# A hybrid decoder layer on one Trainium2 core: mixer B's decode attention as TensorE matmuls

## The chip, the cores and the metric

The kernel runs on one core of one Trainium2 chip. The metric is the device time of one execution in microseconds. A measurement is the median of several executions. The engines are named as the profile names them: PE (TensorE), DVE (VectorE), ACT (ScalarE), POOL (GpSimd) and SP (SyncE, which here only issues transfers).

## The reference, cut to what matters

One layer is run for a prompt of 256 tokens and for 8 decode requests of one token each (264 token columns in all), in fp32.

```python
h = rms_norm(x, g_pre); qA,kA,vA,qB,kB,vB = h @ w_in       # 2048 -> 4352
# mixer A: 16 query heads, 2 kv heads, window 128, sinks
# mixer B: 16 heads of 64, keys at distances 0,d,2d,.. of three branches
DILATIONS = ((128, 1), (512, 4), (2048, 16))
# decode, per request n and head h:
s   = q . k_j / 8          # 320 cached rows and the own one
p   = exp(s - max)         # merged over the branches: a row in c branches counts c times
o_b = sum_j p_j v_j / sum_j p_j
x += rms_norm(concat(rms_norm(o_a), rms_norm(o_b)) @ w_out)
x += rms_norm((gelu(conv3(h2 @ w_gate)) * (h2 @ w_up)) @ w_down)
```

For decode, mixer B needs 8 requests x 16 heads x 321 rows of keys and of values, each row of 64 numbers. Every request and head has keys and values of its own, so there is one query for each set of keys. The count c of a row enters as a table T_MD that is added to the scores.

## The kernel before

**Tiling and stages.** Activations lie transposed: partitions are 128 features, columns the 264 tokens. Weights come as chunks of 128 x 1024 fp32 (512 KB) through a ring of four slots (`raw`). ACT casts a chunk to its high half `wh` (L502), DVE subtracts it to get the low half `wl` (L723), and PE multiplies three times (`mm3`, L1161 to L1163: wh·hh, wh·hl, wl·hh), 24 matmuls of 264 columns per chunk. Chunk n may be loaded when DVE has split chunk n-4. The first 68 chunks are w_in (17 groups of four), the next 16 the half of w_out for mixer B, then come the other half, gate and up, and down.

**The plan.** `make_plan` (driven by the table `STEP`) writes out by hand what happens after which chunk: `PLAN[n]` is a list of steps, and PE, ACT, DVE and POOL each run their part of those steps in that order, one after the other, after chunk n on PE (ACT is three chunks ahead with its casts, DVE two). SP runs the plan six chunks ahead (`AHEAD`), between its weight loads. All engines run their programs strictly in order, so a step that waits holds everything behind it on that engine. `evac` takes a finished group out of PSUM: for t = 0 to 3 the groups qB(t), kB(t), vB(t) (L732 to L735 rotate q and k; L783 scales v), then kvA and qA. `S`, `T`, `V` are the prompt's attention of one head: scores, transposes of the exponentials, times v.

**One bank for small steps.** PSUM bank `B_M` serves all steps listed in `MISC`; a step there waits until the step before it has been copied out (`take_misc`, `misc_free`).

**Mixer B's decode attention, before.** It is done in 8 units u = 2t + v, each of 128 features (two heads) for 8 requests.

- `qk` (PE L1199, ACT L532): q and k of the 8 decode columns are transposed and stored to DRAM (`q_dram`). SP reads q back, broadcast over 128 partitions, into `qb`, and writes the own key into row 64 of the third key block (`qI`, L432 and L434).
- `mul` (POOL L1073): `Kd` (128 rows x 3 blocks x 8 requests x 128 features) times `qb`, in place.
- `bS` (DVE L873): sum over each head's 64 features. `bT` (PE L1287, DVE L880, ACT L574, DVE L884 and L885): three transposes bring the scores to 16 rows x 321; mask, minimum, exponential, and the division.
- `pO`, `pI` (ACT L579, SP L444): the probabilities go to DRAM and come back broadcast over 64 partitions per head, into `Pb`.
- `bM` (POOL L1080, L1082): own value into `Vd`, then `Pb` times `Vd`. `bV` (ACT L585): eight passes with a running sum give `od`, the output by feature and request.

Keys and values come through SP's queue (`load_K` L450 and L451, `load_V` L457), between the weight chunks, and wait there for the step that frees their tile. `aload` (POOL) loads mixer A's caches once the last `bV` is over.

## Time and profile before

| | |
|---|---|
| runs | 1312.35, 1316.21, 1316.63 us; median 1316.21 |
| profiled execution | 1318.04 us, of which the span from first to last instruction is 1316.2 |
| PE busy | 1214.8 us, 92% of the span |
| DVE, ACT, POOL busy | 776.2, 571.0, 203.2 us |
| granted TensorE clock, mean | 0.955 |
| read from HBM | 231 MB, 180 GB/s over the span |

The page cuts the span into 40 slices of 32.9 us. From the 17th slice on PE is busy at 9 tenths or more of each, at full clock. Slices 3 to 16 (66 to 526 us) hold the plan's part and the turn to the FFN; there PE's busy share and its clock move up and down:

```profile
PE   5998777888989897999999999999999999999994
POOL 2053525260200020000101001010010000020003
PEclk9998978888978998999999999999999999999997
```

Each digit is a slice's busy share in tenths; PEclk is the granted clock in tenths of full speed. A busy PE in these rows means that a matmul is under way, not that it runs at its peak.

### The profile page before, as it was taken

What the parts mean: (1) busy time and instruction counts of PE and PEld (TensorE: products, weight loads), DVE (VectorE), ACT (ScalarE), POOL (GpSimd) and SP (SyncE); (2) the same over time, 40 slices, a digit from 0 to 9 for tenths busy, and PEclk for the clock granted to TensorE, in tenths of its full rate; (3) what the DMA queues carried; (4) which work ended last, traced back from release to release, by engine and by line L of the source; (5) the groups of instructions that cost most, each with busy time, mean ns of one, the idle gap of its engine ahead of it and who ended that gap; (6) DMA issues with size and microseconds to landing.
All of it is one profiled execution on the core that took longest, in us unless ns stands there. A gap on an engine that the chain in (4) does not pass through costs nothing.

```text
span 1316.2 us, 24517 instructions
## 1 busy us (share of the span) xinstructions
PE 1214.8 (92%) x9403; PEld 1186.3 (90%) x9403; DVE 776.2 (59%) x993; ACT 571.0 (43%) x938; POOL 203.2 (15%) x134
## 2 busy tenths in 40 slices
PE   5998777888989897999999999999999999999994
PEld 5987776787879897999999999999999999999994
DVE  5657859676554557655655556555565544454445
ACT  4334344436544456544444444444444433343331
POOL 2053525260200020000101001010010000020003
PEclk9998978888978998999999999999999999999997
DMA  6676969695522454455555555555555665656541
GB/s 252 224 242 222 295 195 285 204 255 155 150 75 82 139 172 117 146 184 183 170 168 188 184 182 169 167 189 185 180 171 166 216 185 179 177 181 184 176 144 66
DMA packets 83166, 237.03 MB, mean 180 GB/s; under 512 B 7432, under 2 KB 32368, under 8 KB 82032
## 3 DMA queue, kind: packets, MB, share of 16 engines
q1 hardware_dynamic: 81728, 232.30, 56.9%
q0 software_dynamic: 1072, 3.90, 0.9%
q8 instruction: 31, 0.51, 0.2%
q10 hardware_dynamic: 320, 0.20, 0.1%
q14 instruction: 15, 0.12, 0.0%
HBM read 231.13 MB, written 5.20 MB: 180 GB/s over the span
## 4 chain that ended last, share of the span: by engine, by line
PE 80%; DVE 8%; issue 3%; DMA 3%; ACT 3%; POOL 1%; SPq 0%; ACTq 0%; DVEq 0%; POOLq 0%
PE ps L1161 25%; PE ps L1162 24%; PE ps L1163 24%; DVE wl L723 2%; DMA raw<-in_w_in 2%; DVE bSc L873 1%; DVE bP L885 1%; PE ps L1225 1%; DMA Pb<-p_dram 1%; PE ps L1224 1%; ACT Pb L585 1%; PE ps L1233 1%; DVE sh L734 1%; POOL Kd L1073 1%; DMA qb<-q_dram 1%
## 5 line engine op out<-in xcount | busy, mean ns | idle before, releaser
L1161 PE MATMUL ps<-hh,wh 128*128 128x264 f32 x2080 | 609.3, 293 | 22.0 <-DVE wl L723 16.1
L1163 PE MATMUL ps<-hh,wl 128*128 128x264 f32 x2080 | 601.2, 289 | 0.0
L723 DVE TENSOR_TENSOR wl<-raw,wh 128x1024 fp32r<-128x1024 f32 x364 | 462.8, 1288 | 200.0 <-ACT wh L502 199.8
L1162 PE MATMUL ps<-hl,wh 128*128 128x264 f32 x1952 | 566.3, 290 | 0.0
L502 ACT CAST wh<-raw 128x1024 fp32r<-128x1024 f32 x364 | 375.4, 1045 | 356.9 <-PE ps L1163 298.5
L1161 PEld LDWEIGHTS ps<-hh,wh 128*128 128x128 f32 x2080 | 403.2, 194 | 31.7 <-DVE wl L723 17.5
L1163 PEld LDWEIGHTS ps<-hh,wl 128*128 128x128 f32 x2080 | 401.8, 193 | 0.0
L1162 PEld LDWEIGHTS ps<-hl,wh 128*128 128x128 f32 x1952 | 377.8, 194 | 0.2
L1162 PE MATMUL ps<-gl,wh 128*128 (+1 forms) x704 | 200.4, 285 | 0.0
L1161 PE MATMUL ps<-gh,wh 128*128 (+1 forms) x704 | 199.9, 284 | 0.0
L1163 PE MATMUL ps<-gh,wl 128*128 (+1 forms) x704 | 199.5, 283 | 0.0
L1162 PEld LDWEIGHTS ps<-gl,wh 128*128 128x128 f32 x704 | 132.6, 188 | 0.0
L1161 PEld LDWEIGHTS ps<-gh,wh 128*128 128x128 f32 x704 | 132.5, 188 | 0.0
L1163 PEld LDWEIGHTS ps<-gh,wl 128*128 128x128 f32 x704 | 132.4, 188 | 0.0
L1126 POOL COPY co<-U 128x4 f32 (+1 forms) x22 | 22.1, 1005 | 427.2 <-DVE U L985 427.2
L1073 POOL TENSOR_TENSOR Kd<-Kd,qb 128x3072 f32<-128x3072 f32 x8 | 55.3, 6912 | 59.8 <-DMA qb<-q_dram 59.7
L984 DVE TENSOR_TENSOR U<-ps,rB 128x512 f32<-128x512 f32 x22 | 15.2, 692 | 73.7 <-PE ps L1163 73.7
L1082 POOL TENSOR_TENSOR Pb<-Pb,Vd 128x2568 f32<-128x2568 f32 x8 | 47.3, 5908 | 72.1 <-DMA Pb<-p_dram 72.1
L1004 DVE TENSOR_TENSOR up<-ps,rB 128x528 f32<-128x528 f32 x22 | 15.6, 707 | 69.7 <-PE ps L1163 69.7
L678 ACT ACTIVATE cv<-U,par 128x280 f32<-128x280 f32 x44 | 25.0, 616 | 63.1 <-DVE U L985 63.1
L1233 PE MATMUL ps<-ident,Sm 128*128 128x128 f32 x96 | 18.4, 307 | 32.0 <-ACT Sm L544 31.9
L1142 POOL TENSOR_TENSOR up<-up,ysq 128x528 f32<-128x528 f32 x5 | 9.6, 1917 | 243.2 <-ACT ysq L710 242.7
(210 smaller groups left out, 1085.4 us busy)
## 6 DMA issues: line engine op xcount, KB each, us to landing
raw<-in_w_gate SPq DMA_DIRECT2D x88, 512.0 KB, 3.7
raw<-in_w_up SPq DMA_DIRECT2D x88, 512.0 KB, 4.6
raw<-in_w_down SPq DMA_DIRECT2D x88, 512.0 KB, 3.9
raw<-in_w_in SPq DMA_DIRECT2D x68, 512.0 KB, 6.9
raw<-in_w_out SPq DMA_DIRECT2D x32, 512.0 KB, 3.7
Pb<-p_dram SPq DMA_DIRECT2D x16, 642.0 KB, 8.5
Vd<-in_vb SPq DMA_DIRECT2D x8, 1280.0 KB, 8.5
Kd<-in_kb SPq DMA_DIRECT2D x8, 1024.0 KB, 5.9
```

What stands on the lines that cost most here:

```text
L502: nc.scalar.copy(wh[:, slot], raw[:, slot]).then_inc(hi_ready, 1)
L678: nc.scalar.activation(cv[:, k], U[:, k, 0:NU - 2], ACT.Identity, scale=par[:, bass.ds(i * 2 + (C_CW + k), 1)], bias=par[:, bass.ds(i * 2 ...
L723: V.tensor_tensor(wl[:, slot], raw[:, slot], wh[:, slot].bitcast(F32), ALU.subtract).then_inc(lo_ready, 1)
L984: line.do(V.tensor_tensor(U[:, :, 2:2 + SEQ], ps[:, g:g + 2, 0:SEQ], wide(rB[:, 0:SEQ]), ALU.mult))
L1004: V.tensor_tensor(up[:], ps[:, 2:4, 0:TOK], wide(rB[:]), ALU.mult).then_inc(up_taken, 1)
L1073: G.tensor_tensor(Kd[:], Kd[:], qb[:].unsqueeze(1).to_broadcast([P, 3, NDEC, P]), ALU.mult).then_inc(kq_ready, 1)
L1082: G.tensor_tensor(Pb[:], Pb[:], Vd[:], ALU.mult).then_inc(vp_ready, 1)
L1126: line.do(G.tensor_copy(co[:, bass.ds(i * 2, 2), 0:2], U[:, :, SEQ:SEQ + 2]))
L1161: nc.tensor.matmul(out, a, x, start=start, stop=False)
L1162: nc.tensor.matmul(out, a, xl, start=False, stop=False)
L1163: return nc.tensor.matmul(out, b, x, start=False, stop=stop)
L1233: ins = nc.tensor.transpose(ps[:, B_T, P * c:P * c + P], Sm[:, n % 2, P * c:P * c + P], ident[:])
```

## The change

Each unit's scores and outputs are computed by matmuls on PE, and no product is formed on POOL.

- Host arrays: keys now lie by feature (`kb`: 128 features x 8 requests x 321), values by row in three blocks (`vb`). Keys have two buffers (`Kt`), values one (`Vk`). Both loads are issued by POOL, not SP: `load_K(0)`, `load_V(0)`, `load_K(1)` at step `ss`, `load_K(u+2)` behind `bS(u)`, `load_V(u+1)` behind `bV(u)`.
- `qsel` (POOL): the own key is copied into column 320 of `Kt`; q goes into `Qsel`, a tile that is zero elsewhere. For request 4q + j there is a block of 32 columns in which column 0 holds head 0's q (upper 64 partitions zero) and column 1 head 1's.
- `bS` (PE): for q in 0, 1 and j in 0 to 3 one matmul whose stationary operand is that block (128 x 32) and whose moving operand is the keys of request 4q + j (128 x 321). Position j writes PSUM partitions 32j to 32j+31. q = 1 adds to q = 0: its columns sit two further (blocks are 130 apart, read 128 apart), so rows 32j to 32j+3 hold two requests of two heads. DVE masks and takes the minimum over 128 rows, ACT the exponential.
- `bR` (PE, ACT): three transposes of the 128 x 321 exponentials; copies to `pT`.
- `bV` (PE): for q, three row blocks and j, 24 matmuls: 32 probability columns stationary, the 128 features of request 4q + j's values moving, again at four column positions. ACT scales by the reciprocal sum while copying to `oR`.
- `bO` (PE, ACT): two transposes, then two small strided copies pick the wanted columns into `od`.
- `vdx` (PE, ACT, POOL): the decode columns of v are transposed, copied to `v8`, and sent by DMA into row 64 of the third value block (`load_vself`). It takes the place of `qk` and of the copy `vself`.
- Gone: `q_dram`, `p_dram`, `qb`, `Pb`, `qI`, `mul`, `bT`, `pO`, `pI`, `bM`, SP's part of the plan.

```diff
-    "qI": [-3, 2],
-    "mul": [-2, 4],
-    "bS": [2, 6],
-    "bT": [3, 11],
-    "pO": [3, 11],
-    "pI": [3, 12],
-    "bM": [7, 15],
-    "bV": [8, 16],
+    "qsel": [-3, -3],
+    "vdx": [1],
+    "bS": [-2, 3],
+    "bR": [0, 5],
+    "bV": [2, 7],
+    "bO": [3, 8],
...
             for n in range(4, N_IN):
                 load(chunk(n, 0, 4, 0), d["w_in"][GROUPS[n // 4][2], n % 4])
-                for s in PLAN.get(n - AHEAD, ()):
-                    stage(*s)
...
@@ scalar
+                elif kind == "bR":
+                    act.wait_ge(misc_ready, misc(kind, *a) + 1)
+                    line.do(nc.scalar.copy(pT[:, 0:256], ps[:, B_M, 0:256]))
+                    nc.scalar.copy(pT[0:65, 256:384], ps[0:65, B_M, 256:384]).then_inc(misc_free, 1)
                 elif kind == "bV":
-                    act.wait_ge(vp_ready, u + 1)
-                    for s in range(NDEC):
-                        ins = nc.scalar.activation(Pb[:, s], Pb[:, s], ACT.Identity, accum_out=od[:, 0, u, s:s + 1])
+                    act.wait_ge(misc_ready, misc(kind, *a) + 1)
+                    act.wait_ge(b_rec, u + 1)
+                    nc.scalar.activation(oR[:], ps[:, B_M, 0:256], ACT.Copy, scale=bri[u % 2]).then_inc(misc_free, 1)
...
@@ gpsimd
-                    G.tensor_tensor(Kd[:], Kd[:], qb[:].unsqueeze(1).to_broadcast([P, 3, NDEC, P]),
-                                    ALU.mult).then_inc(kq_ready, 1)
...
-                    G.tensor_tensor(Pb[:], Pb[:], Vd[:], ALU.mult).then_inc(vp_ready, 1)
...
+            def load_K(u):
+                G.dma_start(Kt[:, u % 2], d["kb"][u]).then_inc(Kt_landed[u % 2], 16)
+            def load_V(u):
+                G.dma_start(Vk[:, 0:2], d["vb"][u, :, 0:2]).then_inc(Vk_landed, 16)
+                G.dma_start(Vk[0:64, 2], d["vb"][u, 0:64, 2]).then_inc(Vk_landed, 16)
+            def load_vself(u):
+                v = u % 2
+                G.dma_start(Vk[64:65, 2], v8[:, P * v:P * v + P]).then_inc(Vk_full, 16)
...
@@ tensor
+                elif kind == "bS":
+                    u, = a
+                    pe.wait_ge(qsel_ready, 3 * (u + 1))
+                    take_misc(kind, *a)
+                    v = u % 2
+                    for q in range(2):
+                        for j in range(4):
+                            ins = nc.tensor.matmul(ps[32 * j:32 * j + 32, B_M, 0:KB],
+                                                   Qsel[:, v, P * q + 32 * j:P * q + 32 * j + 32],
+                                                   Kt[:, v, 4 * q + j], start=q == 0, stop=q == 1)
+                    ins.then_inc(misc_ready, 1)
...
+                elif kind == "bV":
+                    u, = a
+                    pe.wait_ge(Vk_landed, 32 * (u + 1))
+                    pe.wait_ge(Vk_full, 16 * (u + 1))
+                    take_misc(kind, *a)
+                    for q in range(2):
+                        for c, (k0, k1) in enumerate(KSPLIT_B):
+                            for j in range(4):
+                                ins = nc.tensor.matmul(ps[32 * j:32 * j + 32, B_M, P * q:P * q + P],
+                                                       pT[0:k1 - k0, P * c + 32 * j:P * c + 32 * j + 32],
+                                                       Vk[0:k1 - k0, c, 4 * q + j], start=c == 0, stop=c == 2)
+                    ins.then_inc(misc_ready, 1)
```

In the plan the numbers are chunks relative to e = 12t + 12, for v = 0 and 1. `vtr` stands at e + 1 too, ahead of `vdx`.

## Rows read from the trace of the kernel before

**Rows 1.** Table of stretches: us, PE, PEld, DVE, ACT, POOL busy, PEclk, DMA, GB/s.

```profile
25.00:320.00 295.00, 245.56 (x1720) 230.05 (x1718) 202.47 (x254) 123.94 (x299) 108.59 (x33) 0.90 0.76 232
57.07:236.69 179.62, 145.03 (x1041) 136.79 (x1040) 132.64 (x149) 72.93 (x173) 79.43 (x23) 0.90 0.82 246
236.69:314.21 77.52, 67.37 (x453) 61.87 (x450) 52.94 (x81) 38.08 (x107) 29.02 (x10) 0.87 0.74 223
```

**Rows 2.** Waits, 25 to 320 us: who <- for whom: us, times, longest.

```profile
ACT wh L502 <- DMA raw<-in_w_in: 36.7, 12, 10.6
PE ps L1233 <- ACT Sm L544: 31.9, 6, 8.8
PE ps L1250 <- ACT PT L552: 9.8, 4, 3.5
PE ps L1161 <- DVE wl L723: 2.1, 1, 2.1
```

**Rows 3.** Timeline, 211 to 224 us: start, us, instruction, [idle before].

```profile
212.07 6.71 POOL L1073 TENSOR_TENSOR Kd<-Kd,qb 128x3072 f32<-128x3072 f32 x1 [2.56 <-DMA qb<-q_dram]
212.16 7.18 DVE L734 SCALAR_TENSOR_TENSOR sh<-sh,tab 128x528 f32<-128x528 f32 x1
...
222.86 0.90 PE L1233 MATMUL ps<-ident,Sm 128*128 128x128 f32 x3 [8.80 <-ACT Sm L544]
```

**Rows 4.** Groups by line and shape, 25 to 320 us: xcount | busy, mean ns | idle before.

```profile
L723 DVE TENSOR_TENSOR wl<-raw,wh 128x1024 fp32r<-128x1024 f32 x57 | 91.9, 1620 | 27.8 <-ACT wh L502 27.7
...
L1073 POOL TENSOR_TENSOR Kd<-Kd,qb 128x3072 f32<-128x3072 f32 x8 | 55.3, 6912 | 59.8 <-DMA qb<-q_dram 59.7
L1082 POOL TENSOR_TENSOR Pb<-Pb,Vd 128x2568 f32<-128x2568 f32 x7 | 41.6, 5944 | 43.8 <-DMA Pb<-p_dram 43.8
...
L585 ACT ACTIVATE Pb<-Pb 128x321 f32<-128x321 f32 x56 | 25.5, 458 | 4.6 <-POOL Pb L1082 4.6
```

**Rows 5.** Table of stretches, two chunks behind a pause or small matmuls.

```profile
172.30:177.40 5.10, 5.10 (x28) 5.10 (x27) 1.22 (x1) 4.70 (x14) 0.00 (x0) 0.57 0.49 190
392.70:398.10 5.40, 5.40 (x25) 5.40 (x26) 0.58 (x2) 1.37 (x3) 0.00 (x0) 0.50 0.37 97
```

**Rows 6.** Timeline of PE, 113 to 122 us, one small step after another.

```profile
113.06 0.48 PE L1224 MATMUL ps<-ks,qs 64*128 64x128 f32 x2
...
113.91 0.39 PE L1161 MATMUL ps<-hh,wh 128*128 128x264 f32 x1
...
116.94 0.49 PE L1233 MATMUL ps<-ident,Sm 128*128 128x128 f32 x3
...
117.27 0.44 PE L1287 MATMUL ps<-ident,bSc 128*16 128x128 f32 x3
...
117.52 0.37 PE L1161 MATMUL ps<-hh,wh 128*128 128x264 f32 x1
...
120.53 0.33 PE L1250 MATMUL ps<-vn,PT 128*128 128x64 f32 x2
...
121.11 0.37 PE L1161 MATMUL ps<-hh,wh 128*128 128x264 f32 x1
```

**Rows 7.** Timeline, 126 to 128 us: v's transposes and ACT's copy of them.

```profile
126.07 0.66 PE L1209 MATMUL ps<-ident,vT 128*128 128x128 f32 x4 [1.75 <-DVE vself L784]
...
126.48 0.37 PE L1161 MATMUL ps<-hh,wh 128*128 128x264 f32 x1
...
126.76 0.59 ACT L521 COPY vn<-ps 128x512 f32<-128x512 f32 x1 [0.27 <-PE ps L1209]
```

**Rows 8.** DMA issues: out<-in, queue, xcount, KB each, median us from issue to landing.

```profile
Vd<-in_vb SPq DMA_DIRECT2D x8, 1280.0 KB, 8.5
...
VtA<-in_va POOLq DMA_DIRECT2D x1, 512.0 KB, 6.2
...
VtA<-vdec POOLq DMA_DIRECT2D x1, 4.0 KB, 3.3
```

**Rows 9.** The chain that ended last, in order of time: start, us, what.

```profile
113.54 0.43 PE ps L1225 x2
...
390.24 2.45 PE ps L1259 x32
```

More of the change, by code:

```diff
@@ L49 @@
 SUMS = MT // 2
-AHEAD = 6
 OUT_V = 5
@@ L144, in make_plan @@
         gap = STEP["gap"][t]
-        add(e + STEP["qk"][0], "qk", t)
         add(e + 1, "vtr", t)
+        add(e + STEP["vdx"][0], "vdx", t)
         for a in range(4):
@@ L194 @@
 MISC = [s for n in sorted(PLAN) for s in PLAN[n]
-        if s[0] in ("ss", "qk", "vtr", "vdec", "aS", "aT", "aR", "aV", "W", "ND", "bT")]
+        if s[0] in ("ss", "vtr", "vdx", "vdec", "aS", "aT", "aR", "aV", "W", "ND", "bS", "bR", "bV", "bO")]
 def number(kind, *args):
@@ L333, in build @@
         amn, al, aes, ari = (small[:, c:c + 1] for c in (74, 75, 76, 77))
-        bmn, bl, bri = (small[0:16, c:c + 1] for c in (78, 79, 80))
+        bmn, bl = (small[:, c:c + 1] for c in (78, 79))
+        bri = [small[:, c:c + 1] for c in (80, 81)]
         sinkn = small[:, 82:82 + H_A + 1]
@@ L365, in build @@
         KtA_landed, VtA_landed, VtA_full = sem("KtA_landed"), sem("VtA_landed"), sem("VtA_full")
-        Kd_landed, Kd_full, Vd_landed = sem("Kd_landed"), sem("Kd_full"), sem("Vd_landed")
-        q_out, qb_landed, p_out, Pb_landed = sem("q_out"), sem("qb_landed"), sem("p_out"), sem("Pb_landed")
-        kq_ready = sem("kq_ready")
-        bS_ready, bV_ready = sem("bS_ready"), sem("bV_ready")
-        vp_ready = sem("vp_ready")
+        Kt_landed = [sem(f"Kt_landed{c}") for c in range(2)]
+        Vk_landed, Vk_full = sem("Vk_landed"), sem("Vk_full")
+        qsel_ready = sem("qsel_ready")
         norm_a = sem("norm_a")
@@ L781, in evac @@
                         dve.wait_ge(v_stored, 16 * t)
-                        dve.wait_ge(misc_ready, misc("vtr", t - 1) + 1)
-                    line.step(V.tensor_tensor(vT[:], src, wide(rB[:]), ALU.mult))
-                    V.tensor_copy(vself[:, t], vT[:, :, SEQ:TOK]).then_inc(evac_done, 1)
+                        dve.wait_ge(misc_ready, misc("vdx", t - 1) + 1)
+                    V.tensor_tensor(vT[:], src, wide(rB[:]), ALU.mult).then_inc(evac_done, 1)
             def stage(kind, *a):
@@ L869, in stage @@
                     u, = a
[L870 to L876 removed]
                     dve.wait_ge(misc_ready, misc(kind, *a) + 1)
                     if u:
[L879 removed]
+                        dve.wait_ge(b_exp, u)
                     V.tensor_tensor_reduce(
[L881 removed]
+                        out=bSm[:], in0=ps[:, B_M, 0:KB], in1=tab[:, T_MD:T_MD + KB], scale=1.0, scalar=NEG,
                         op0=ALU.add, op1=ALU.min, accum_out=bmn).then_inc(misc_free, 1)
                     dve.wait_ge(b_exp, u + 1)
[L884 to L885 removed]
+                    V.reciprocal(bri[u % 2], bl).then_inc(b_rec, 1)
                 elif kind == "N":
```

194 lines of the change are left out of this document (85 added, 109 removed).

## The prediction

> **What bounds the kernel now.** I read the table of stretches first. In the 295.0 us from 25 to 320, where the w_in groups and mixer B's decode attention run together, PE is busy 245.6 us, so it sits idle 49.4 us at a granted clock of 0.90 [rows 1]. Afterwards the diff touches little. Next came PE's waits there: nearly all of the idle time ends with the exponential or the P^T copy on ACT (31.9 and 9.8 us), and ACT in turn sits 36.7 us until weights land [rows 2]. Neither is slow work. The timeline shows where ACT's delay starts: POOL's multiply of keys by q runs from 212.07 for 6.71 us, a rotate step on DVE that starts 0.09 us later takes 7.18 us, and PE then waits 8.80 us [rows 3]. So while POOL multiplies two SBUF tiles, a DVE instruction can stand still until it ends. The subtraction that makes the low weight half (L723) has a mean of 1620 ns in the stretch, a mix of free and held ones. POOL spends 55.3 and 41.6 us in the two multiplies [rows 4]. After such a pause PE also pays in clock: the chunk from 172.30 takes 5.10 us at a granted clock of 0.57, so mostly at 1.2 of the two levels 1.2 and 2.4 GHz [rows 5].
>
> How much is that together? A chunk (24 matmuls of 264 columns) at full clock goes from 117.52 to 120.53, 3.01 us. A head's S costs 0.85 (113.06 to 113.91), its T 0.33 (116.94 to 117.27), its V 0.58 (120.53 to 121.11), unit u's bT 0.25 (117.27 to 117.52) [rows 6]; four transposes (vtr; qk taken alike) 0.4 (126.07 to 126.48) [rows 7]. From 57.07 to 236.69 lie 36 chunks, 12 heads, 3 vtr and 3 qk, and 6 bT: 108.4 + 21.1 + 2.4 + 1.5 = 133.4 us. The window is 179.6, so 46.2 us are lost. From 236.69 to 314.21 lie 14 chunks, 8 S, 7 T, 7 V, 1.1 us of vtr and qk, and 3 bT: 57.1 of 77.5 us, 20.4 lost [rows 1]. **66.6 us** in all are idle time or low clock. PE's early wait for weights (2.1 us) [rows 2] I leave in place: before, keys and values go ahead of the weights in SP's queue, after it 3.9 MB (K0, V0, K1) share the engines with them from POOL's queue.
>
> **The change, part by part.** (1) *Multiplies, sums and broadcasts go.* POOL loses both multiplies, DVE the reduction bSc and the scaling of bP, ACT the eight accumulating passes per unit (25.5 us in seven units [rows 4]), the queues the broadcast reads of q and P. None of these engines is PE, so their own time is worth nothing; what they free is the 66.6 us. What is late next is PE itself, and I count the 66.6 in full: in a stretch without POOL's multiply on DVE's way (109 to 116) PE goes from chunk to chunk without a wait [rows 6].
>
> (2) *SP's queue* loses its waits (bS_ready, q_out, p_out, vp_ready), so weights no longer queue behind them: a gain that is part of (1). The loads themselves (two or three DMAs per unit, plus v's own row) go to POOL's queue, past its stores of k and v; nothing on POOL but its small copies waits behind them, and (6) prices the one that is late.
>
> (3) *PE's small steps.* Gone: 8 bT x 0.25 and 4 qk x 0.4, 3.6 us. New: 8 bR of three 128-column transposes x 0.33 (like T), 2.6; 8 bO of two x 0.22 (two thirds of that), 1.8; 4 vdx of two x 0.2, 0.8. Net **+1.6 us**.
>
> (4) *PE's big steps, where the trace has no such row.* bS is 8 fp32 matmuls of 321 moving columns, bV 24 of 128. An fp32 matmul leaves two records: two of 256 columns take 0.43 us on the chain [rows 9], 0.84 ns per column and record. One record of bS is then 0.27 us, one of bV 0.107. Upper end, if column positions do not run beside each other: 16 x 0.27 + 48 x 0.107 = 9.4 us per unit, 75.5 in all. Lower end, if all four run at once: a quarter, 2.35 per unit, 18.8 in all. Between them: the two records of one matmul stand next to each other in PE's order and use the same position, so the second must wait for the first, while the next position's first record can run beside the second. That gives (8 + 1) x 0.27 + (24 + 1) x 0.107 = 5.1 us per unit, **41** in all. A second row speaks for that size even if positions overlap fully: 32 records of only 16 columns take 2.45 us [rows 9], 77 ns each where streaming can't be the limit, and 48 such are 3.7 us for bV, with 1.2 to 2.4 for bS. I take 41.
>
> The Trainium skill, page "TensorEngine Tiling (Array Packing)", Tiling Modes, says that tiles operate independently and that different tiles execute weight loads and matmuls in parallel; by it the sum would hold the lower end. No row of before has a column position, so the trace neither agrees nor disagrees. "TensorE: Matmul & The Clock Gate", Part 3, gives 2.38x for three column positions, and says that matmuls start and end in program order, which is why I don't take the quarter.
>
> (5) *One bank for all of it.* B_M holds one small step at a time. vdx now follows vtr in the same plan step, so PE waits for ACT's copy, 0.59 us plus a hop [rows 7]: 0.75 x 4. bO(2t) is followed by bS(2t+1): two copies, 0.7 x 4. bR(7) by vtr(4): 0.75. Together **6.6 us**, and ACT's casts queue behind nothing new.
>
> (6) *v's own row.* load_vself(2t) is issued by POOL after vdx, one plan step before bV(2t) wants it on PE. The like DMA (4 KB from vdec) landed 3.3 us after issue [rows 8]; with copy, wait and issue 4.1 us after vdx, against a chunk of 3.01 and a head's S of 0.85 that PE has in between. It also stands in POOL's queue behind K(2t+2), 1.3 MB; 512 KB there took 6.2 us, the load before it included [rows 8], so I put 1.3 MB at some 9, and it was issued about 10 earlier. Bounds 0 (landed) and 4 us each; I take 1.5 x 4 = **6**. Queued behind the wait on PE are all chunks; POOL's wait for vdx holds only the next loads. Some of these waits end in a slow chunk, 2.1 us each [rows 5]: two of them, **4**.
>
> (7) *Hidden:* POOL's three small copies per unit (Qsel and the key column) lie a step ahead of bS; the memset of Qsel is over before x lands; DVE loses the memset of Kd; V and K prefetches have five or more chunks (over 15 us) against 8.5 us for the 1280 KB of Vd [rows 8]. If that cover failed, PE would wait 1 to 3 us per unit.
>
> Sum: -66.6 + 1.6 + 41 + 6.6 + 6 + 4 = **-7.4 us**. The profiled execution spans 1316.2 (1318.0 with what lies around it) and the median of the runs is 1316.2, so the same time: **1308.8 us**.
>
> **The rivals.** *A. Column positions don't overlap* (that the change doesn't do what it says): 34.5 us more than the forecast, 1343, slower. It decides above about 6.0 us per unit for bS and bV. For: fp32 streams at half the rate of the weight chunks' matmuls, so a limit in reading the operand may bind already. Against: nothing in the rows. *B. Full overlap:* 22 us less, 1287. Against: the 77 ns per record, and two records per matmul. *C. The clock falls behind the new stretches.* Behind the 2.45 us of 16-column matmuls the chunk from 392.70 took 5.40 us at 0.50, so 1.2 GHz [rows 5]. If a 32-wide stretch does the same, each of 16 costs 2 us: +32, 1341, slower. Against: the new matmuls stream 128 and 321 columns. *D. Weight loads at column positions aren't hidden.* "TensorE: Matmul & The Clock Gate", Part 3, says that weight loads overlap running matmuls only with another row group, and all positions here have the same. As a mechanism of this kernel: 64 records per unit that each wait for a load of about 77 ns [rows 9] add 4.9 us to the 9.4, so 39 us beyond rival A, 1382. The chunks speak against it: their loads, also all rows, are hidden in 24 matmuls per 3.01 us [rows 6].
>
> **How the numbers follow.** Forecast 0.44, A 0.20, B 0.21, C 0.12, D 0.03. The forecast's own range, 1297 to 1321, comes from (5) and (6) (6 to 29 us where I took 17) and from 4 to 6 us per unit in (4). The range reaches to B and A: **1285 to 1343**, which leaves out about half of A, D and a third of B. A measurement here tells 0.3%, 4 us, from no change. Faster: B 0.21 and two thirds of the forecast 0.30, 0.51. Same: 0.13. Slower: A, C, D and the rest, 0.36.
>
> **What would show it.** In the profile after: no DVE instruction stretched to 4 or more us before 320; PE idle there under 20 us instead of 49; bS of 2.4 us and bV of 2.7 between their first record and the next chunk (4.3 and 5.1 under A, 1.1 and 1.3 under B); PE's waits naming ACT's copies and Vk, each under 2 us; no slow chunk behind bS or bV (C). A chunk that waits for weights would mean that POOL's bulk loads crowd them out, and the 66.6 is then not all gained. It would be wrong above all if bS and bV take another time than 5.1 us per unit: each us there is 8 us.

## The result, and the profile after

After the change the kernel takes **1276.3 us** (median; 1274.8 to 1277.0) against 1314.3 (1312.0 to 1316.6) of the kernel before on the same chip: a ratio of 0.971, 95% interval 0.969 to 0.973. Two more series gave 0.969 (0.966 to 0.972) and 0.971 (0.968 to 0.974). The forecast of 1308.8 had the right sign and a fifth of the gain: 7 us were forecast, 38 measured, and the time lies below the range, nearest to rival B. The profiled executions span 1316.2 and 1274.7 us, 41.5 apart.

The table of stretches of the kernel after comes first (columns as in [rows 1]). The second row holds the same 50 chunks as the last two of [rows 1] together (57.07 to 314.21), counted from the start of the program: the first of them starts at 57.51 before and at 54.22 after.

```profile
25.00:320.00 295.00, 280.89 (x2468) 255.79 (x2467) 145.22 (x294) 127.22 (x276) 31.15 (x70) 0.98 0.59 200
54.22:279.55 225.33, 215.96 (x2014) 196.34 (x2012) 106.04 (x212) 96.10 (x212) 28.83 (x66) 0.99 0.64 213
```

Where the kernel before had PE idle for 49.4 of 295 us at a clock of 0.90, it is now idle for 14.1 at 0.98. What took 257.1 us (57.07 to 314.21) takes 225.3, although PE has all of the new matmuls in it. Two single chunks answer to [rows 5]: the one slow chunk that is left up to 279.55, at a clock of 0.66, and the chunk right behind the first scores, at full clock.

```profile
251.57:256.10 4.53, 4.53 (x28) 4.53 (x27) 1.23 (x1) 1.32 (x2) 0.00 (x0) 0.66 0.53 144
58.92:61.97 3.05, 3.05 (x29) 3.05 (x26) 2.19 (x5) 1.60 (x3) 0.53 (x1) 1.00 0.77 272
```

PE's waits, 25 to 290 us (who, for whom, us in all, times, longest), answer to [rows 2]:

```profile
PE ps L1262 <- ACT od L533: 3.6, 4, 1.7
PE ps L1172 <- ACT vn L466: 3.1, 4, 0.8
PE ps L1181 <- ACT pT L521: 1.8, 1, 1.8
PE ps L1295 <- DVE onat L829: 1.5, 1, 1.5
PE ps L1136 <- DVE wl L673: 1.4, 1, 1.4
PE ps L1205 <- ACT Sm L484: 0.6, 1, 0.6
PE ps L1281 <- issue: 0.5, 1, 0.5
PE ps L1262 <- POOL Qsel L1025: 0.4, 1, 0.4
```

The 31.9 us for the exponential are gone (0.6). The first three rows are waits for the bank B_M: bS (L1262) behind ACT's copy of the turned output, vdx (L1172) and vtr (L1181) behind ACT's other copies. The row for L1281 is bV of unit 4, at 178.77; no releaser is named for it, but it is v's own row: its DMA was issued at 175.18 and landed 3.5 us later, at 178.68. Two timeline rows show it, the first of POOL, the second of PE:

```profile
175.18 0.52 POOL L1067 DMA_DIRECT2D Vk<-v  x1 [6.30 <-ACT v L475]
...
178.77 0.38 PE L1281 MATMUL ps<-Vk,pT 128*32 128x128 f32 x5 [0.52 <-issue]
```

ACT's wait for weights (36.7 us in [rows 2]) and the group of the low weight half (1620 ns in [rows 4]) are, 25 to 320 us:

```profile
ACT wh L447 <- DMA raw<-in_w_in: 12.4, 4, 9.7
```

```profile
L673 DVE TENSOR_TENSOR wl<-raw,wh 128x1024 fp32r<-128x1024 f32 x64 | 77.5, 1219 | 21.0 <-ACT wh L447 20.9
```

1219 ns is the time of a subtraction that nothing holds up. The disputed cost, last: PE's timeline (start, us, instruction, in brackets the idle time before it) around the first scores and the first values.

```profile
57.70 1.29 PE L1262 MATMUL ps<-Kt,Qsel 128*32 128x321 f32 x16 [0.41 <-POOL Qsel L1025]
58.92 0.39 PE L1136 MATMUL ps<-hh,wh 128*128 128x264 f32 x1
...
74.07 1.52 PE L1281 MATMUL ps<-Vk,pT 128*32 128x128 f32 x48
75.52 0.39 PE L1136 MATMUL ps<-hh,wh 128*128 128x264 f32 x1
```

From the first record to the next chunk pass 1.22 us for scores and 1.45 for values, the same in all eight units: 2.67 us a unit, 21.4 in all, where the forecast had 41 and rival A 75.5. The values' matmuls alone (L1281; us, PE busy and records under way, PEld, clock) begin as a wave of four records, one for each position, and the next four join 0.11 us later:

```profile
74.06:74.17 0.11, 0.10 (x4) 0.10 (x8) 1.00 0.54 223
74.17:74.28 0.11, 0.11 (x8) 0.11 (x12) 1.00 0.92 372
```

### The profile page after: what moved, and what is told of

It is laid out like the page before. It is cut to its first block, busy times and chain, and to the rows that moved or that the text cites. A ratio compares the mean times of both kernels' runs of the same rounds, so it can differ in the third digit from the quotient of the medians.

```text
span 1274.7 us, 25414 instructions
## 1 busy us (share of the span) xinstructions
PE 1212.9 (95%) x9923; PEld 1178.8 (92%) x9923; DVE 692.5 (54%) x972; ACT 550.9 (43%) x850; POOL 118.0 (9%) x167
## 4 chain that ended last, share of the span: by engine, by line
PE 91%; DVE 3%; issue 2%; ACT 1%; POOL 0%; DVEq 0%; ACTq 0%; POOLq 0%
PE ps L1136 28%; PE ps L1137 27%; PE ps L1138 27%; PE ps L1197 1%; PE ps L1196 1%; PE ps L1281 1%; PE ps L1205 1%; PE ps L1262 1%; PE ps L1165 1%; PE ps L1318 1%; PE ps L1224 1%; PE ps L1223 1%; DVE yT L980 1%; DVE yT L981 1%; PE ps L1222 0%
## 5 line engine op out<-in xcount | busy, mean ns | idle before, releaser
L1136 PE MATMUL ps<-hh,wh 128*128 128x264 f32 x2080 | 602.2, 290 | 20.7 <-DVE wl L673 14.9
L1137 PE MATMUL ps<-hl,wh 128*128 128x264 f32 x1952 | 559.4, 287 | 0.0
L673 DVE TENSOR_TENSOR wl<-raw,wh 128x1024 fp32r<-128x1024 f32 x364 | 441.4, 1229 | 193.3 <-ACT wh L447 193.1
L1136 PEld LDWEIGHTS ps<-hh,wh 128*128 128x128 f32 x2080 | 395.9, 190 | 33.0 <-issue 17.0
L1138 PEld LDWEIGHTS ps<-hh,wl 128*128 128x128 f32 x2080 | 394.7, 190 | 0.0
L1137 PEld LDWEIGHTS ps<-hl,wh 128*128 128x128 f32 x1952 | 370.8, 190 | 0.2
L929 DVE SCALAR_TENSOR_TENSOR cv<-U,par,cv 128x280 f32<-128x280 f32 x88 | 41.0, 506 | 10.0 <-ACT cv L628 6.8
L638 ACT CAST gh<-up 128x528 f32 (+1 forms) x22 | 14.0, 634 | 73.3 <-DVE up L947 73.3
L482 ACT ACTIVATE Sm<-Sm,small 128x128 f32<-128x128 f32 x32 | 12.9, 402 | 72.7 <-DVE small L764 72.7
L1136 PE MATMUL ps<-oBh,wh 128*128 128x264 f32 x128 | 40.5, 316 | 0.0
```

Source lines behind the costliest of these rows:

```text
L482: line.do(nc.scalar.activation(Sm[:, p, 0:P], Sm[:, p, 0:P], ACT.Exp, scale=-1.0, bias=mn[:, T % 2, 0, h:h + 1], accum_out=ll[:, T % 2, 0, ...
L638: nc.scalar.copy(gh[:, bass.ds(i * 2, 2)], up[:]).then_inc(gh_ready, 1)
L673: V.tensor_tensor(wl[:, slot], raw[:, slot], wh[:, slot].bitcast(F32), ALU.subtract).then_inc(lo_ready, 1)
L929: ins = V.scalar_tensor_tensor(cv[:, k], U[:, k, tap:tap + NU - 2], par[:, bass.ds(i * 2 + (C_CW + FT * tap + k), 1)], cv[:, k], ALU.mult, ...
L1136: nc.tensor.matmul(out, a, x, start=start, stop=False)
L1137: nc.tensor.matmul(out, a, xl, start=False, stop=False)
```

## The experiments

Beside the first of them the kernel after was timed again, with its expectation:

> The kernel after, timed again as the mark for the runs beside it: 1275 to 1277 us, 0.971 of before.

It took 1277.5 us (1273.5 to 1278.6). Three questions follow, in this order: what the column positions give, where the 66.6 us came from, and what the one bank costs. Theory P (positions): all four run beside each other nearly in full. Its rival is the forecast's own rule, that only neighbours in PE's order overlap.

**No column positions.**

```diff
-ins = nc.tensor.matmul(ps[32 * j:32 * j + 32, B_M, 0:KB],
-                       Qsel[:, v, P * q + 32 * j:P * q + 32 * j + 32],
+ins = nc.tensor.matmul(ps[:, B_M, 0:KB],
+                       Qsel[:, v, P * q:P * q + P],
```

and the like for the values. Expected:

> No column positions: every score and value matmul of mixer B's decode takes the whole 128-column stationary block and writes all 128 partitions of the bank, 8 matmuls for scores and 24 for values as before. The blocks of other requests are added up, so B's decode attention is left wrong and out of the computation; the work is the same in number and columns. Nothing can overlap: by the rows of after, waves are 0.27 us apart (scores) and 0.107 us (values), and each wave held four records; one record a wave gives 16 x 0.27 = 4.3 us and 48 x 0.107 = 5.1 us a unit against 1.22 and 1.45. Theory overlap (four positions share PE's time nearly whole): 1276.3 + 8 x (3.1 + 3.7) = 1330. Rival: positions contribute little and the records are short for another reason: 1276 to 1290.

Measured: 1330.5 us (1326.4 to 1332.3), as theory overlap had it, and 1.1% above before (ratio 1.011, 1.008 to 1.014). The timeline of PE around unit 1's scores and values:

```profile
88.91 4.57 PE L1262 MATMUL ps<-Kt,Qsel 128*128 128x321 f32 x16 [0.53 <-ACT od L533]
93.07 0.53 PE L1136 MATMUL ps<-hh,wh 128*128 128x264 f32 x1
...
108.63 5.62 PE L1281 MATMUL ps<-Vk,pT 128*128 128x128 f32 x48
114.01 0.37 PE L1136 MATMUL ps<-hh,wh 128*128 128x264 f32 x1
```

The same 16 and 48 records take 4.16 and 5.38 us: 9.5 a unit, as rival A had computed (9.4). Rival A's condition was thus well priced, and it isn't met. Without the positions the change would have been a loss of 1%.

The granted clock fell in two of these sixteen stretches: the scores of the first and of the last unit take 5.88 and 5.85 us, and PE had been idle for 1.89 and 1.71 us just before them. The first stood at a clock of 0.71.

**Two positions of 64 columns in place of four of 32.**

```diff
-ins = nc.tensor.matmul(ps[32 * j:32 * j + 32, B_M, 0:KB],
-                       Qsel[:, v, P * q + 32 * j:P * q + 32 * j + 32],
+ins = nc.tensor.matmul(ps[64 * (j % 2):64 * (j % 2) + 64, B_M, 0:KB],
+                       Qsel[:, v, P * q + 64 * (j % 2):P * q + 64 * (j % 2) + 64],
```

> Two column positions of 64 in place of four of 32, the same number of matmuls and columns; two requests' blocks are added up in each half, so B's decode attention is not computed. Theory overlap by positions: two at a time, so scores 8 x 0.27 = 2.2 us and values 24 x 0.107 = 2.6 us a unit, + 2.1 in all: 1276.3 + 8 x 2.1 = 1293. If the forecast's own rule held (only the second record of one and the first of the next overlap), two positions would be as good as four: 1276 to 1280. If nothing overlapped with 64 columns: 1330.

Measured: 1295.6 us (1294.3 to 1296.6); by the same timeline scores take 2.31 and values 2.78 us in a unit at full clock, 5.1 in all. Four, two and one position give 2.67, 5.1 and 9.5 us: PE's time is shared out by the number of positions, within 12% of the ideal at four. The forecast's rule, by which two would do as well as four, falls.

**The positions outermost.**

```diff
-for q in range(2):
-    for c, (k0, k1) in enumerate(KSPLIT_B):
-        for j in range(4):
+for j in range(4):
+    for q in range(2):
+        for c, (k0, k1) in enumerate(KSPLIT_B):
```

and j outside q for the scores.

> The same matmuls of scores and values with the loop over the column positions outermost, so that the two (scores) or six (values) matmuls of one position follow each other. Theory order (that of the prediction): matmuls start in program order, and the next starts beside the last only where its position is another one; with the positions outermost only the last matmul of one position and the first of the next run side by side. Then 16 records of scores take 16 x 0.27 - 3 x 0.27 = 3.5 us instead of 1.22, 48 of values take 48 x 0.107 - 3 x 0.107 = 4.8 us instead of 1.45 (0.27 and 0.107 us are the distances between the waves of four in the trace of after), and the time rises by 8 x (2.3 + 3.4) = 45 us: about 1321. Rival queues: each position works off its own matmuls and others are handed out past a busy one, so that the order plays no part: 1275 to 1278.

Measured: 1297.9 us (1295.7 to 1299.3), between both, and 20.4 above after on the same chip; the values' matmuls alone would make it 8 x 2.7 = 21.7. The scores don't mind (1.24 us), the values do (4.16 us, against 1.45). A table of stretches of the values' matmuls alone (L1281; us, PE busy and records in each, PEld, clock) shows when positions start:

```profile
74.78:75.68 0.90, 0.89 (x8) 0.89 (x9) 1.00 0.86 332
75.68:76.59 0.91, 0.91 (x14) 0.91 (x13) 1.00 0.56 198
```

For 0.90 us one position works alone: eight records, one every 0.11 us. Then its ninth record and the first of the next position start together, and a record that is under way at the edge counts in both rows. Of a position's 12 records the last three were then still to start. The scores have four records a position, so the second position starts at once. So neither theory holds whole: the positions do work off their records beside each other, but those of the next position were held up for as long as more than three records of the busy one had yet to start. That suggested the next run.

**Three matmuls of one position in a row.**

```diff
 for q in range(2):
-    for c, (k0, k1) in enumerate(KSPLIT_B):
-        for j in range(4):
+    for j in range(4):
+        for c, (k0, k1) in enumerate(KSPLIT_B):
```

> The values' loop with the three pieces of keys inside the position (q, then position, then piece), so that three matmuls, six records, of one position follow each other, where after has one and the kernel with the positions outermost had six. Theory queue: a position takes up to four records behind one another, and only the fifth holds up those behind it; by that the score matmuls (two in a row, four records) lost nothing with the positions outermost, 1.24 us, and with six in a row each next position began eight records late. With three in a row the next begins two records late: 12 waves of 0.109 plus 3 x 2 waves, about 2.0 us at most and 1.6 at least (the second q runs on behind the first) against 1.45: + 1 to 5 us, 1277 to 1281. Rival no queue: a row of three costs nearly what a row of six costs, 3.5 us a unit or more: 1292.

Measured: 1284.4 us (two executions, 1282.2 and 1286.6), 3 above the expected 1277 to 1281. The values' matmuls in stretches of 0.25 us, and the timeline:

```profile
74.32:74.57 0.25, 0.24 (x3) 0.25 (x3) 1.00 0.76 246
74.57:74.81 0.24, 0.24 (x7) 0.24 (x6) 1.00 0.72 284
74.81:75.06 0.25, 0.25 (x11) 0.25 (x8) 1.00 1.12 459
```

```profile
74.33 2.58 PE L1281 MATMUL ps<-Vk,pT 128*32 128x128 f32 x48
76.84 0.39 PE L1136 MATMUL ps<-hh,wh 128*128 128x264 f32 x1
```

The next position starts right behind the third of six records, every 0.25 us: again three are left to start. So the starts don't keep the program's order. Each position's fifth and sixth record are of the third piece of keys, which has 65 rows; by the program's order two of the first six starts would be such records, and none is (L1281, 74.3 to 74.78: median ns, first and last start, forms):

```profile
L1281 PE MATMUL ps<-Vk,pT x6: 272/272/297, 74.3 to 74.7; 128*32 128x128 f32 x6
```

The values take 2.51 us, 0.5 more than I had given as the most, because the second q doesn't run on behind the first: its four positions start 0.25 us apart as well. Theory queue stands, its rival (3.5 us) falls; the depth it states, "four", is one record at work and three waiting. How PE holds them isn't in the trace; only the starts are.

**The scores twice.**

```diff
-for q in range(2):
+for q in (0, 1, 0, 1):
```

> Each of the 8 units' score matmuls is issued twice into the same bank (the result is the same): 8 x 8 more matmuls. Theory PE-bound: the stretch is PE's, so the second pass costs what the first takes, 8 x 1.22 = 9.8 us: about 1286. Rival slack: the stretch is bound by the weights' transfers and by the split on DVE, PE has room: 1276 to 1279. The rival of the prediction by which a pass of eight costs 4.3 us would give 1311.

Measured: 1287.4 us (1286.4 to 1289.0), 9.9 to 11.1 above after. The second pass is on the path at its full price, so the stretch is PE's after the change: each us of bS and bV is 8 us of the kernel, as the prediction said. In six units both passes take 2.30 us together at full clock. In the first and the last unit, behind 1.90 and 1.71 us of idle time, they take 3.99 at a lower granted clock (the first; columns as in [rows 1]):

```profile
57.72:61.71 3.99, 3.99 (x32) 1.37 (x33) 0.00 (x0) 0.00 (x0) 0.58 (x3) 0.57 0.66 249
```

The second question: **which of the removed things made the idle time?** Four kernels cut the kernel before.

**POOL's products cut.**

```diff
-G.tensor_tensor(Kd[:], Kd[:], qb[:].unsqueeze(1).to_broadcast([P, 3, NDEC, P]),
+G.tensor_tensor(Kd[:, 0, 0, 0:8], Kd[:, 0, 0, 0:8], qb[:, 0, 0:8],
                 ALU.mult).then_inc(kq_ready, 1)
...
-G.tensor_tensor(Pb[:], Pb[:], Vd[:], ALU.mult).then_inc(vp_ready, 1)
+G.tensor_tensor(Pb[:, 0, 0:8], Pb[:, 0, 0:8], Vd[:, 0, 0:8], ALU.mult).then_inc(vp_ready, 1)
```

> The kernel before with POOL's two large products (K times q, P times V) cut to 8 columns of one block, so B's decode attention is not computed; all DMAs, DVE's sums and every wait stay. It asks which part of the 66.6 us that the forecast took back from idle time and the half clock came from POOL's products, which held up DVE's fp32 subtractions beside them. Theory POOL: nearly all of it, time falls by 45 to 65 us: 1251 to 1271. Rival transfers: the broadcast reads and the late weights are the cause, DVE's long instructions only lie beside them: it falls by 0 to 15 us: 1300 to 1316. In between, both have a share.

Measured: 1285.6 us (1278.6 to 1291.6), 30 less: in between. Rows of its waits and its group of the low weight half, 25 to 320 us:

```profile
ACT wh L502 <- DMA raw<-in_w_in: 69.9, 20, 13.0
...
PE ps L1233 <- ACT Sm L544: 28.5, 6, 11.8
```

```profile
L723 DVE TENSOR_TENSOR wl<-raw,wh 128x1024 fp32r<-128x1024 f32 x61 | 74.0, 1218 | 55.7 <-ACT wh L502 55.6
```

The subtraction is at its free 1218 ns, yet PE's wait for the exponential hardly moves (31.9 to 28.5), and ACT's wait for weights doubles (36.7 to 69.9). With DVE free, the weights' transfers are what is late. (The profiled execution was the slowest of the four, 1291.6 us, so these rows show the least of the gain.)

**Broadcasts to fewer partitions.**

```diff
-sp.dma_start(qb[:], q_dram[...].unsqueeze(0).to_broadcast([P, NDEC, P])
+sp.dma_start(qb[0:16], q_dram[...].unsqueeze(0).to_broadcast([16, NDEC, P])
...
-sp.dma_start(Pb[64 * h:64 * h + 64], src.to_broadcast([64, NDEC, KB])).then_inc(Pb_landed, 16)
+sp.dma_start(Pb[64 * h:64 * h + 16], src.to_broadcast([16, NDEC, KB])).then_inc(Pb_landed, 16)
```

> The kernel before with the broadcast reads of q and of P written to 16 and 2 x 16 partitions in place of 128 (the rest of the tiles holds zeros, so B's decode attention is not computed): an eighth and a fourth of their traffic, all products and waits stay. Theory POOL: POOL's products make the idle time: the time falls by 0 to 15 us: 1300 to 1316. Rival transfers: ACT's waits for weights (36.7 us in the stretch before, 12.4 after) come from this traffic, and they are what PE's idle time is made of: it falls by 20 to 50 us: 1265 to 1295.

Measured: 1307.6 us (1295.4 to 1310.1, ratio 0.992, 0.990 to 0.995), 8 less, as theory POOL had it. Alone, the traffic is worth little: POOL's products are still there, and PE now waits for DVE's subtraction 10.8 us where it was 2.1 in [rows 2]:

```profile
PE ps L1163 <- DVE wl L723: 10.8, 5, 3.9
```

**Both cuts.**

> The kernel before with both cuts: POOL's two large products at 8 columns of one block, and the broadcast reads of q and P into 16 and 2 x 16 partitions (B's decode attention is not computed; all waits, DVE's sums and the loads on SP stay). Alone the first gave 30 us and the second 8 us. Theory two bounds in series: the products hold DVE, the transfers hold the weights, and whichever is left alone keeps most of the idle time, so both together give more than the sum of 38: 50 to 66 us, 1250 to 1266. Rival sum: they give 38 and no more, 1278, and the rest of the 66.6 us is DVE's two passes over the products and the waits between stages, which only the change takes away.

Measured: 1264.9 us (1259.5 to 1269.8), 49 less than before on the same chip (ratio 0.963, 0.956 to 0.970), where 30 and 8 alone make 38. So each cut hides some of the other, though it is just short of the first theory's 50 to 66. The medians alone don't prove it: their 95% intervals reach 5 and 4 us to each side for the single cuts and 9 for both. The profiles below say the same more clearly: PE's idle time falls by 9.0 and by 4.4 us with one cut, by 25.5 with both.

**Both cuts, and the sums over the products.** DVE's reduction to one block, ACT's eight accumulating passes to one:

```diff
-V.tensor_reduce(bSc[:], Kd[:].rearrange("p c s (h e) -> p (c s h) e", h=2), AX.X,
+V.tensor_reduce(bSc[:, 0:2], Kd[:, 0, 0].rearrange("p (h e) -> p h e", h=2), AX.X,
...
-for s in range(NDEC):
-    ins = nc.scalar.activation(Pb[:, s], Pb[:, s], ACT.Identity, accum_out=od[:, 0, u, s:s + 1])
+ins = nc.scalar.activation(Pb[:, 0], Pb[:, 0], ACT.Identity, accum_out=od[:, 0, u, 0:1])
```

> The kernel before with both cuts (POOL's products, the broadcast traffic) and with the sums over the products cut as well: DVE's reduction (3.35 us a unit) to one block and ACT's eight sums (0.65 us each) to one, so B's decode attention is not computed; all waits between the stages stay. Theory sums: the open 17 us are these instructions between DVE's splits and ACT's casts: the time falls from 1265 to 1248 or so (66.6 under before), at most 1245. Rival waits: the steps left in line (queries out and back through memory, the one bank) hold PE, and it stays at 1260 to 1265.

Measured: 1249.3 us (1247.6 to 1252.6) against 1314.4: **65 us less**, so theory sums stands. The stretch 25 to 320 us of the four kernels, in the order products cut, broadcasts cut, both, both and the sums (one row from each; columns as in [rows 1]):

```profile
25.00:320.00 295.00, 254.59 (x1850) 237.58 (x1848) 165.46 (x291) 136.52 (x329) 15.05 (x34) 0.92 0.83 243
```
```profile
25.00:320.00 295.00, 250.04 (x1778) 233.61 (x1777) 220.61 (x279) 130.71 (x314) 110.66 (x34) 0.92 0.66 201
```
```profile
25.00:320.00 295.00, 271.08 (x2004) 253.27 (x2003) 183.17 (x335) 152.83 (x376) 16.20 (x38) 0.96 0.70 215
```
```profile
25.00:320.00 295.00, 278.39 (x2082) 260.32 (x2081) 166.25 (x354) 134.38 (x278) 16.90 (x38) 0.97 0.71 217
```

PE's idle time goes from 49.4 us [rows 1] to 40.4, 45.0, 23.9 and 16.6. No single one of the three is "the" bound. The last kernel keeps every matmul of the kernel before, and shows what the 50 chunks of the 66.6 us take without lost time (from their first chunk on):

```profile
61.13:251.46 190.33, 189.14 (x1490) 179.17 (x1487) 109.25 (x230) 89.09 (x180) 13.75 (x33) 1.00 0.87 267
```

Before, the same 1490 records took 256.7 us (57.51 to 314.21), 66.4 more.

**Products put into the kernel after.** 14 products of 2112 elements that nobody needs:

```diff
+def idle_product(u, k):
+    pool.wait_ge(qsel_ready, 3 * nq[0])
+    G.tensor_tensor(oBh[:], oBh[:].bitcast(F32), oBl[:].bitcast(F32), ALU.mult).then_inc(scr_done, 1)
+    pool.wait_ge(scr_done, 3 + k)
```

> The kernel after with 14 products put on POOL that nobody needs (oBh times oBl, 2112 fp32 elements a partition, behind the loads of K and of V of each unit; the computation is whole). Before, products of 3072 elements took 6.71 us on POOL beside a DVE that took 7.18 us for a subtraction; 2112 elements scale to 4.6 us, 14 of them to 65 us. Theory POOL alone: products hold up DVE's splits and PE waits for them, as far as before: taking them out of the kernel before gave 30 us, so 65/94 of that, + 21: about 1297. Rival both together: a held-up split is made up by the chunks ahead as long as the weights come early, as they do after the change: 1277 to 1283.

Measured: 1286.3 us (1283.5 to 1292.2), some 10 above after as timed on other chips. One product and DVE beside it, then the group of the low weight half:

```profile
61.33 4.74 POOL L1085 TENSOR_TENSOR oBh<-oBh,oBl 128x2112 fp32r<-128x2112 f32 x1
...
61.77 6.52 DVE L675 TENSOR_TENSOR wl<-raw,wh 128x1024 fp32r<-128x1024 f32 x2
```

```profile
L675 DVE TENSOR_TENSOR wl<-raw,wh 128x1024 fp32r<-128x1024 f32 x62 | 96.8, 1572 | 16.2 <-ACT wh L448 15.9
```

Two subtractions take 6.52 us where 2.44 would do, and the mean goes from 1219 back to 1572 ns, without any of the old traffic. So a DVE instruction stands still beside POOL's product; with weights landing early half of the scaled 21 us is made up, and half is not.

**Loads on SP again.** SP issues K, V and v's own row six chunks ahead, waiting as it did before:

```diff
-G.dma_start(Kt[:, u % 2], d["kb"][u]).then_inc(Kt_landed[u % 2], 16)
+sp.dma_start(Kt[:, u % 2], d["kb"][u]).then_inc(Kt_landed[u % 2], 16)
```

> The kernel after with the loads of K, V and v's own row issued by SP, in the plan six chunks ahead and between the weights' loads, as before the change, and not by POOL. SP then waits for the scores or values to be done before it issues such a load, and the weights' loads behind it wait with it. Theory queue: a part of the 66.6 us came from SP being held: 1276.3 + 10 to 30. Rival: SP is six chunks ahead and has room: 1276 to 1279.

Measured: 1274.4 us (1274.1 to 1274.7). After was not timed on this chip; elsewhere it took 1276.3 to 1277.5. Moving the loads to POOL's queue gave nothing; SP does as well. The waits for q and P that SP had before (`q_out`, `p_out`) are not in this kernel, since it has no such transfers.

The third question: **the one bank.** The stages get steps of their own, so that none follows on the bank of the last:

```diff
-    "vdx": [1],
-    "bS": [-2, 3],
-    "bR": [0, 5],
-    "bV": [2, 7],
-    "bO": [3, 8],
+    "vdx": [2],
+    "bS": [-2, 5],
+    "bR": [0, 7],
+    "bV": [3, 8],
+    "bO": [4, 9],
...
-    add(53, "vtr", 4)
-    add(54, "vdec")
+    add(54, "vtr", 4)
+    add(58, "vdec")
```

> Mixer B's decode stages get steps of the plan of their own, so that none opens with a wait for the one PSUM bank B_M that the stage before it still holds. In the trace of after, PE waits for that bank (for ACT's copy of the turned output 3.6 us, for the copy of v 3.1 us, for the copies of P 1.8 us) 8.5 us in all. Theory bank: these waits are on the path and go: 1276.3 - 8.5 = about 1268, at the least 1271 if the weights' waits take a third of the room. Rival weights: in this stretch PE works at the pace at which DVE and ACT split and cast the weights, and waits of 0.5 us are made up by the queue of chunks ahead: 1275 to 1277. Rival lateness: the output two to three chunks later is in nobody's way; if it were, PE would wait at the next unit's scores, and the time rises by 1 to 3 us.

Measured: **1264.1 us** (1262.4 to 1267.5), ratio to before 0.960 (0.957 to 0.963), and 13.4 less than after on the same chip. The longest of PE's waits, 25 to 290 us:

```profile
PE ps L1262 <- POOL Qsel L1025: 1.8, 1, 1.8
```

The three rows for the bank are gone (the wait for Qsel has grown from 0.4 to 1.8 us), and with them more than their 8.5 us: behind the wait of 1.8 us that ended at 251.26 the chunk of 4.53 us stood at a clock of 0.66 in the kernel after, 1.5 us over a free one, and it is not there any more.

> The kernel with stages at steps of their own, timed again beside after on one chip: 1264 against 1276, 13 us less (8.5 us of waits for the bank, 4 to 5 us of the half clock that PE had behind the last of them).

Again 1262.2 us against 1276.8 of after, timed beside it:

> The kernel after, timed beside the others on the same chip as their mark: 1276 to 1278 us.

So the gain of 13 to 15 us holds. Waits and that chunk make 10 of it. The same stretch of 49 chunks, in after and then in this kernel, differs by 11.6 us:

```profile
58.92:279.55 220.63, 211.67 (x1976) 193.06 (x1972) 102.95 (x208) 93.77 (x210) 26.09 (x59) 0.99 0.64 212
```
```profile
58.79:267.85 209.06, 208.51 (x1976) 191.00 (x1972) 103.05 (x208) 94.12 (x210) 28.09 (x59) 1.00 0.69 224
```

A wait costs more than its idle time, because the record ahead of it runs out alone: between the starts of the last bO record and the next bS lie 0.80 us at 79.28 where 0.52 are idle, and 0.03 us from bO to the next chunk at 101.46, where nothing waits. What is left, 2 to 3 us, differs from run to run: behind these chunks the first of the two profiles takes 2.4 us less than that of after, with less half clock, and the second takes the same. With the loads on SP on top of it:

> Both edits at once: the stages at steps of their own, and the loads of K and V issued by SP. If the 2 us that the loads on SP gave (1274.4) are real and come from elsewhere than the bank's waits, this is 1262; if they came from those waits or from the spread of the runs, 1264.

1261.5 us (1258.4 to 1265.3): no different from 1262.2. The best version is the one with steps of their own, 4% under before.

## Why the prediction was wrong, point by point

**(1), (2) The 66.6 us: right in size.** Cutting what POOL, DVE, ACT and the queues did for mixer B's decode, with nothing put in its place, gave 65 us, and in the 50 chunks that the 66.6 were counted from it gave 66.4. The story behind it was too simple: I had named POOL's hold on DVE as the start of it all. Products alone gave 30, traffic alone 8, both 49, and the sums another 16. The lost time of a stretch could be counted from its rows; its cause couldn't be read off one episode [rows 3]. What (2) called a part of the gain, SP's queue, is hardly one: with the loads and their waits back on SP the kernel after loses nothing, and the kernel that keeps all of SP's waits, those for q and P too, still gave the 66.4.

**(3) Small steps: +1.6.** Right within 1 us: in the kernel with own steps, where they don't wait, the new ones take 4.5 us in all (5.2 booked), and those gone took 3.5 in the same chunks before.

**(4) bS and bV: the step that failed.** 41 us were booked, 21.4 measured. The price of a record without overlap was right (9.4 us a unit against 9.5 measured). What failed is the rule for the overlap: I let each position's second record wait for its first and gave only the neighbour credit. In fact the four positions start together, one wave each 0.11 us, and both records of one matmul follow each other at that pace on their position while the other three work. The program's order, position innermost, never put more than two records of one position in a row. The support from 77 ns a record [rows 9] was misleading too: 48 records at 77 ns are 3.7 us, and they took 1.45, so 77 ns is no floor under every record. Those of [rows 9] all write from partition 0, so they share one position; why they take 77 ns isn't shown. The lower end (2.35 a unit) was 12% short of 2.67. The records show positions that run in parallel. The Trainium skill, page "TensorEngine Tiling (Array Packing)", Tiling Modes, says so, and the trace agrees (four records in the first wave). The other reason that the prediction gave against the quarter was the order of starts: the Trainium skill, page "TensorE: Matmul & The Clock Gate", Part 3, has matmuls start and end strictly in program order. For the starts the trace with three matmuls of one position in a row disagrees (no 65-row record among its first six), and the trace decides. Order does matter, but as far as records of one position pile up: 1.45, 2.51 and 4.16 us for two, six and twelve in a row.

**(5) The bank: right mechanism, 6.6 booked.** The rows named as forecast (bS for od, vdx for vn, vtr for pT) add up to 8.5 us of idle time, and the one slow chunk makes it 10. By the runs with own steps the arrangement costs 11.6 us in this stretch, and 13 to 15 by the medians. The prediction listed these collisions and priced them, but took them as part of the change.

**(6) v's own row and two slow chunks: 10 booked, 0.5 of the first and one of the second (1.5) found.** The mechanism is there, but in one unit of four: PE waited 0.52 us for the row of unit 4, 4.5 us after the last record of vdx. The DMA issues of the kernel after (KB each, median us from issue to landing):

```profile
Kt<-in_kb POOLq DMA_DIRECT2D x8, 1284.0 KB, 6.0
...
Vk<-v POOLq DMA_DIRECT2D x8, 4.0 KB, 5.2
```

K takes 6.0 us where I had put 9. The rows that the term is about, of units 0, 2, 4 and 6, landed 1.6, 2.2, 3.5 and 2.5 us after issue; the median of 5.2 is raised by those of the odd units, which stand behind the loads of V.

**The sum.** For the 50 chunks, with what was measured in place of what was booked: -66.6 + 1.6 + 21.4 + 8.5 + 0.5 (v's row) + 1.5 (the slow chunk) = -33.1; the two profiles differ by 257.1 - 225.3 = 31.8. The forecast was 24.4 off there: (4) made 19.6 of it and (6) with the slow chunks 8.0, while (5) went 1.9 the other way, and 1.3 more, open, went that way too. The rest of the gain, 41.5 - 31.8 = 9.7, lies outside: 2.9 us ahead of these chunks, where the prediction left PE's early wait "in place", and 6.8 behind them, where it looked for nothing ("afterwards the diff touches little"). One row of the kernel before and one of after hold the same 495 matmul records:

```profile
314.21:400.00 85.79, 75.04 (x495) 67.18 (x494) 44.16 (x115) 46.07 (x119) 7.50 (x5) 0.84 0.38 102
```
```profile
279.55:360.00 80.45, 72.76 (x495) 64.76 (x494) 42.38 (x114) 40.74 (x98) 0.00 (x0) 0.87 0.24 80
```

5.3 us less: 3.1 of idle time (10.7 to 7.7) and 2.3 of busy time with the same records at a higher clock. POOL's last product (7.50 us of POOL here) is gone; how much of this is its doing isn't shown. Another 1.5 us lies further on.

**The rivals.** A (no overlap): refuted by the timeline. The kernel without positions meets its condition and took 1330, not 1343: its matmuls cost 4 us more than A's 75.5 (the two scores at a clock of 0.71), of the 10 us of (6) only a wait of 0.6 is there, and what it had lost up to the end of the 50 chunks, 23.0 us, was 12.5 at the end of the program. B (full overlap, 1287): the nearest, 21 of 100 given to it; still 11 too high, for the reasons in (6) and the 9.7 us outside the stretch. The sign that the prediction gave for it, 1.1 and 1.3 us a unit, came within 0.15 us (1.22 and 1.45). Its odds should have been the higher ones: against it spoke a duration from matmuls on one position, which can't tell how positions share. C (clock): in the profile of after no chunk behind bS or bV is slow; behind the first scores it is 3.05 us at 1.00. So C is not what happened. Where scores did run at a lower clock, PE had waited just before: 1.7 to 1.9 us in the two units each of the kernels without positions and with the scores twice, and 1.71 us for the bank in after timed again, whose last scores took 2.30 us instead of 1.22. The units between, with 0.7 us or less of idle time, kept the full clock. But the same wait of 1.71 us left the last scores at full clock in the profile of after, so a wait alone doesn't decide it. (After timed again, columns as in [rows 1].)

```profile
239.67:241.97 2.30, 2.29 (x16) 0.66 (x16) 0.00 (x0) 0.00 (x0) 0.00 (x0) 0.50 0.11 29
```

D (weight loads at column positions not hidden): refuted. 48 records with their loads take 1.45 us, 30 ns each, where a load alone lasts 109 ns, not the 77 that the prediction took from the records of [rows 9] (group of the values' weight loads of the kernel after, 25 to 320 us):

```profile
L1281 PEld LDWEIGHTS ps<-Vk,pT 128*32 128x32 f32 x256 | 6.7, 109 | 2.4 <-issue 2.2
```

The Trainium skill, page "TensorE: Matmul & The Clock Gate", Part 3, lists that loads overlap running matmuls only with another row group (its description of the mechanism also allows a load into the background weight buffer). All positions here have the same rows, so this trace disagrees with the listed rule, and the trace decides.

## What to carry to other kernels

Small matmuls at four column positions cost little more than a quarter of what they cost on one, if the loop over the positions is innermost; with six records of one position in a row a quarter of the gain was lost (2.51 us, between 1.45 and 5.38), with twelve two thirds (4.16). Before a range is drawn, look for the term with the most uncertain price and the largest count: here 1 us in one unit was 8 us of the kernel. The case that only a distant row spoke against was the nearest one here. And where a change takes several things off several engines at once, count the lost time of the stretch as a whole, since one cut alone shows less than half of it; then give every user of a shared bank a step of its own, which was worth another 13 us here. And before two profiles are compared stretch by stretch, count the chunks in both stretches: the same clock time held 50 of them in one kernel and 49 in the other.

## What the runs showed of the hardware

- fp32 matmuls with 32 stationary columns at four positions start as a wave of four, one wave each 0.11 us for 128 moving columns; 16 records of 321 columns take 1.22 us (4.16 without positions) and 48 of 128 take 1.45 (5.38).
- A position seems to take one record at work and three waiting before the matmuls behind are held up: the next position started once all but three records of the last had started, with 12 (0.90 us), 6 (0.25 us) and 4 in a row (at once). Records of the next position thus start ahead of those that the program has before them.
- A POOL product of 2112 fp32 elements (4.74 us) stretches two DVE subtractions beside it from 2.44 to 6.52 us, nearly by its own length, without any of the old traffic.
- A wait on PE costs more than its idle time: 0.80 us from start to start with 0.52 idle, where 0.03 would do.
- Scores ran at a lower granted clock (0.57 in 3.99 us, 0.71 in 5.88, 0.50 in 2.30) only where PE had been idle for 1.7 to 2.1 us just before, and not each time; behind 0.7 us or less it stayed at 1.00.
